# Hyena filters on Trainium2: forward and backward weights multiplied once each in two row halves of the array, their sum and difference made by VectorE

## The reference, cut to what matters

```python
def hyena_filters(L, w1, b1, w2, b2, w3, freq):
    ...
    h = (h @ w3.astype(F32)).reshape(L, HY_ORDER, 2, D_MODEL)
    ...
    return h * window[:, None, None, :]

def two_sided_fft_conv(u, h_fwd, h_bwd, bias):
    L = u.shape[1]
    kern = jnp.concatenate([h_fwd, jnp.zeros((1, h_fwd.shape[1]), F32), h_bwd[:0:-1]], axis=0)
    uf = u.astype(F32)
    spec = jnp.fft.rfft(uf, n=2 * L, axis=1) * jnp.fft.rfft(kern, n=2 * L, axis=0)[None]
    y = jnp.fft.irfft(spec, n=2 * L, axis=1)[:, :L]
    return (y + uf * bias.astype(F32)).astype(u.dtype)

def hyena_mixer(h, w_in, b_in, short_w, short_b, w1, b1, w2, b2, w3, freq, filt_bias, w_out, b_out):
    ...
    filt = hyena_filters(L, w1, b1, w2, b2, w3, freq)
    z = x1 * two_sided_fft_conv(v, filt[:, 0, 0], filt[:, 0, 1], filt_bias[0])
    z = x2 * two_sided_fft_conv(z, filt[:, 1, 0], filt[:, 1, 1], filt_bias[1])
    return z @ w_out + b_out
```

## Time and profile before

| | us |
|---|---|
| time, median of 3 runs | 2646.16 |
| lowest and highest of them | 2643.12, 2646.53 |
| the profiled execution, its own time | 2648.7 |
| span of the profiled execution | 2646.3 |
| mean granted TensorE clock, share of full speed | 0.969 |
| PE busy over the span | 2461.9 (93%) |
| DVE busy over the span | 1141.1 (43%) |
| ACT busy over the span | 773.5 (29%) |

### The profile page before, as it was taken

One profiled execution on the slowest core, in us unless ns is written; L12 is line 12 of the kernel. 1 busy time (PEld: TensorE's weight loads), 2 busy tenths in 40 slices (PEclk: granted clock), 3 DMA queues, 4 the chain that ended last, 5 costly groups with the idle time before them and its releaser, 6 DMA issues. The chain is left out here.

```text
span 2646.3 us, 39564 instructions
## 1 busy us (share of the span) xinstructions
PE 2461.9 (93%) x16812; PEld 1555.6 (59%) x16812; DVE 1141.1 (43%) x2226; ACT 773.5 (29%) x1602; POOL 51.5 (2%) x68
## 2 busy tenths in 40 slices
PE   8989999999899999978799999998999969988887
PEld 7856888888678888855443334344767743322222
DVE  4456543333788989886300000002556542211113
ACT  4346433333433333223311111112347522110002
POOL 0000000000000000000200000000000010000000
PEclk9979999999999999987899999999999979999999
DMA  5240332222210101025799999997230479999996
GB/s 205 97 153 29 143 116 96 96 96 96 94 50 33 50 33 50 32 112 203 313 383 397 377 384 386 393 384 320 101 159 2 191 258 367 428 428 428 427 428 284
DMA packets 58103, 570.49 MB, mean 216 GB/s; under 512 B 6815, under 2 KB 15015, under 8 KB 24776
## 3 DMA queue, kind: packets, MB, share of 16 engines
q1 hardware_dynamic: 50904, 544.37, 51.5%
q0 software_dynamic: 5584, 18.35, 2.2%
q10 hardware_dynamic: 1440, 5.24, 0.5%
HBM read 554.84 MB, written 13.11 MB: 215 GB/s over the span
## 5 line engine op out<-in xcount | busy, mean ns | idle before, releaser
L2973 PE MATMUL moe_gate<-ring,moe_xe_l 128*32 128x512 f32 (+1 forms) x1240 | 192.6, 599 | 17.8 <-DMA ring<-in_moe_gu 11.9
L3960 DVE SCALAR_TENSOR_TENSOR moe_hidden<-moe_hidden,moe_gate_rows,moe_up 128x512 f32<-128x512 f32 x31 | 23.2, 747 | 400.4 <-ACT moe_hidden L3883 400.4
L2973 PE MATMUL moe_up<-ring,moe_xe_l 128*32 128x512 f32 (+1 forms) x1240 | 190.2, 594 | 0.0
L3988 DVE SCALAR_TENSOR_TENSOR residual<-experts_psc,mod,residual 128x512 f32<-128x512 f32 (+1 forms) x76 | 53.3, 707 | 283.9 <-PE experts_psc L3824 169.1
L3744 PE MATMUL experts_py_l<-ring,experts_turn_l 128*32 128x512 f32 (+1 forms) x1136 | 141.3, 593 | 3.5 <-DMA ring<-in_moe_down 2.8
L1019 DVE TENSOR_TENSOR mlp_w_lo<-ring,mlp_w_hi 128x512 fp32r<-128x512 f32 x144 | 96.7, 688 | 97.8 <-ACT mlp_w_hi L964 97.6
L3883 ACT ACTIVATE moe_hidden<-moe_gate 128x512 f32<-128x512 f32 x31 | 18.5, 597 | 360.2 <-PE moe_up L2973 360.2
L964 ACT CAST mlp_w_hi<-ring 128x512 fp32r<-128x512 f32 x144 | 86.4, 618 | 123.5 <-PE mlp_acc L920 123.5
L2973 PEld LDWEIGHTS moe_up<-ring,moe_xe_l 128*32 128x32 f32 (+1 forms) x1240 | 49.7, 115 | 108.2 <-issue 108.2
L2973 PEld LDWEIGHTS moe_gate<-ring,moe_xe_l 128*32 128x32 f32 (+1 forms) x1240 | 44.8, 115 | 99.9 <-issue 70.1
L918 PE MATMUL mlp_acc<-mlp_h_hi,mlp_w_hi 128*128 128x512 f32 x256 | 100.0, 391 | 0.0
(11 more groups left out here) (678 smaller groups left out, 5210.5 us busy)
## 6 DMA issues: line engine op xcount, KB each, us to landing
ring<-in_moe_gu SPq DMA_DIRECT2D x91, 2048.0 KB, 11.3
ring<-in_moe_down SPq DMA_DIRECT2D x45, 2048.0 KB, 9.8
ring<-in_ada_w SPq DMA_DIRECT2D x24, 2048.0 KB, 8.6
ahead_wide_early<-in_moe_gu SPq DMA_DIRECT2D x9, 2048.0 KB, 30.5
ahead_wide_high<-in_moe_gu SPq DMA_DIRECT2D x9, 2048.0 KB, 30.5
ahead_wide_low<-in_moe_gu SPq DMA_DIRECT2D x9, 2048.0 KB, 30.4
normed<-in_moe_gu SPq DMA_DIRECT2D x9, 2048.0 KB, 30.5
ring<-in_w_up SPq DMA_DIRECT2D x8, 2048.0 KB, 7.4
```

Of the source, the lines that this page charges most:

```text
L2973: last = core.nc.tensor.matmul(banks[m][at:at + n, :], xe_l[:, e, k, a:a + n], columns(2 * kk + m, FH * half, FH), start=(k == 0), stop=(k ...
```

## The change: one product per side, and the sum and difference on DVE

`w3` now holds the forward weights in rows 0 to 63 and the backward weights in rows 64 to 127, once each. `filters` takes two tiles at a time: four matmuls of 64 rows by 256 columns, of which those of the upper rows write the forward side into one bank and those of the lower rows the backward side into another. `turn_filters_round` and one DMA a turn are gone. `make_taps` multiplies two banks by the window for each pair of tiles, and the new `sides` makes sum and difference in place: the first instruction adds the backward side to the forward one, the second takes twice the backward side from that sum, the third adds the bias to one row.

```diff
-        w3 = st.sb("w3", [P, 2, 2, QC])
+        w3 = st.sb("w3", [P, 2, QC])
...
-        win_loaded = st.counter("hy_win_loaded", 96 * TURNS)
+        win_loaded = st.counter("hy_win_loaded", 80 * TURNS)
...
-                        sp.wait_ge(sp_free.handle, sp_free.at(4 + spec_at(q - 1, 18 + 5)))
+                        sp.wait_ge(taps_made.handle, taps_at(q - 1, 1, 4))
...
-                        sp.dma_start(w3[0:64, :, s, :], last_layer[:, :, 0, :]).then_inc(win_loaded.handle, 16)
-                    sp.dma_start(w3[64:P, :, 0, :], last_layer[:, :, 1, :]).then_inc(win_loaded.handle, 16)
+                        sp.dma_start(w3[64 * s:64 * (s + 1), :, :], last_layer[:, :, s, :]).then_inc(win_loaded.handle, 16)
...
                 def filters(it, o, some=range(6)):
-                    for t in some:
-                        b = take_spec(it, 18 * o + t)
-                        nc.tensor.matmul(b[:], h2[:, t * P:(t + 1) * P], w3[:, o].rearrange("p s n -> p (s n)"), start=True, stop=True).then_inc(sp_done.handle, 1)
-
-                def transform(it, m0, src):
+                    for t in some[::2]:
+                        both = [take_spec(it, 18 * o + t + s) for s in range(2)]
+                        for i in range(2):
+                            for s in range(2):
+                                side = slice(64 * s, 64 * (s + 1))
+                                last = nc.tensor.matmul(both[s][:, i * QC:(i + 1) * QC], h2[side, (t + i) * P:(t + i + 1) * P], w3[side, o, :], start=True, stop=True, tile_position=(64 * s, 0))
+                                if i:
+                                    last.then_inc(sp_done.handle, 1)
+
+                def transform(it, m0, src, made):
...
+                            if a == 0 and s in made:
+                                pe.wait_ge(taps_made.handle, made[s])
...
                 def spectra(it, o):
-                    pe.wait_ge(sp_free.handle, sp_free.at(4 + spec_at(it, 18 * o + 5)))
-                    transform(it, 18 * o + 6, lambda a: taps[:, a])
+                    transform(it, 18 * o + 6, lambda a: taps[:, a], {0: taps_at(it, o, 0), 2: taps_at(it, o, 4)})
...
-                turn_filters_round(0)
...
-                        turn_filters_round(it + 1)
...
                 def make_taps(it, o, some=range(6)):

-                    for t in some:
+                    for t in some[::2]:
                         m = 18 * o + t
-                        if t == 5:
-                            dve.wait_ge(sp_free.handle, sp_free.at(4 + spec_at(it, m - 1)))
-                            if o:
-                                dve.wait_ge(win_loaded.handle, win_loaded.at(96 * (it + 1)))
-                            zero = taps[0:1, 0, 0:5:4, :]
-                            link(nc.vector.tensor_tensor(zero, zero, at_zero[:].unsqueeze(1).to_broadcast([1, 2, QC]), ALU.add))
-                        dve.wait_ge(sp_done.handle, sp_done.at(spec_at(it, m)))
-                        nc.vector.tensor_tensor(taps[:, :, t, :], spec[m % 4][:].rearrange("p (s n) -> p s n", s=2), win[:, t].unsqueeze(1).to_broadcast([P, 2, QC]),
-                                                ALU.mult).then_inc(sp_free.handle, 1)
+                        dve.wait_ge(sp_done.handle, sp_done.at(spec_at(it, m + 1)))
+                        for s in range(2):
+                            last = nc.vector.tensor_tensor(taps[:, s, t:t + 2, :], spec[(m + s) % 4][:].rearrange("p (t n) -> p t n", t=2), win[:, t:t + 2, :], ALU.mult)
+                            last.then_inc(sp_free.handle, 1)
+
+                def sides(it, o, first, n):
+
+                    dve.wait_ge(sp_free.handle, sp_free.at(4 + spec_at(it, 18 * o + first + n - 1)))
+                    ahead, behind = [taps[:, s, first:first + n, :] for s in range(2)]
+                    link(nc.vector.tensor_tensor(ahead, ahead, behind, ALU.add))
+                    link(nc.vector.scalar_tensor_tensor(out=behind, in0=behind, scalar=-2.0, in1=ahead, op0=ALU.mult, op1=ALU.add))
+                    dve.wait_ge(win_loaded.handle, win_loaded.at(80 * (it + 1) if o else 80 * it + 64))
+                    zero = taps[0:1, 0, first, :]
+                    nc.vector.tensor_tensor(zero, zero, at_zero[:], ALU.add).then_inc(taps_made.handle, 1)
...
                         make_taps(0, 0)
+                        sides(0, 0, 0, 4)
+                        sides(0, 0, 4, 2)
...
                         add_out(it - 1, 5)
+                        sides(it, 0, 0, 4)
                         add_out(it - 1, 6)
+                        sides(it, 0, 4, 2)
                         add_out(it - 1, 7)
...
                     make_taps(it, 1, range(4))
+                    sides(it, 1, 0, 4)
                     convolve(it, 4)
                     convolve(it, 5)
                     make_taps(it, 1, range(4, 6))
+                    sides(it, 1, 4, 2)
```

More of the change, by code:

```diff
@@ L2311, in spec_at, with taps_at @@
             return it * SP + m + 1
+        def taps_at(it, o, first):
+            return taps_made.at(4 * it + 2 * o + (2 if first else 1))
         def out_chunk(it):
@@ L2496, in _ @@
                     if it == 0:
-                        pe.wait_ge(turned_round.handle, turned_round.at(1))
+                        pe.wait_ge(win_loaded.handle, win_loaded.at(64))
                         filters(0, 0)
@@ L2645, in gated_high @@
                         nc.scalar.copy(u_hi[:, j, 0:UP - 2], u[:, 4 + j, 0:UP - 2]).then_inc(u_high.handle, 1)
-                def turn_filters_round(it):
-                    act.wait_ge(win_loaded.handle, win_loaded.at(96 * it + 80))
-                    nc.scalar.activation(w3[64:P, :, 1, :], w3[64:P, :, 0, :], ACT.Identity, scale=-1.0).then_inc(turned_round.handle, 1)
                 weights_high(-1, 0)
```

8 lines of the change are left out of this document (4 added, 4 removed).

## The result

The changed kernel takes 2656.6 us (median of 6 runs, 2655.4 to 2659.1) against 2646.0 (6 runs, 2639.1 to 2650.5): slower, ratio 1.0042 (95% interval 1.0028 to 1.0055), 10.6 us. The forecast was 2655.1, 8.9 us slower.

The account below looks back on a forecast made before the run. PE and DVE were taken to hand the lead to each other, DVE's slack being 3.05 + 3.49 us in turn 1. Turns 0 to 3 add 2.9 + 2.1 + 2.5 + 1.4 = +8.9 to 2646.2: 2655.1 us, range 2653.0 to 2660.6.

Parts of the forecast that it names:

- Prices: Filters of four tiles 2.1 us on PE, of two 1.25; `sides` 2.84 and 1.78 on DVE; linked steps 1.25 and 0.72.
- DVE's waits used up, the rest passed on to PE: Beside the outward products, turns 1 to 3: 3.79 us more on DVE against 3.05 of waits; second transposes 1.6 later.
- ACT's cast: At the turn's end: outward products wait for this cast, so about 0.5 of PE's 1.3 us filter saving arrives.
- The clock: PE's clock falling at three new waits, 1.5 us each; counted only in the upper end of the range.
- Turn 0: +2.9 us at the turn's end, +3.9 if the third pair of tiles waits for banks at a slow clock.
- PE's lead: Turn 0, first order: gates wait 2.08 us for PE, so its 1.3 saving counts and +2.0 reaches the second order.
- Turn 3: +1.4 us: 1.6 - 1.31 in the first order, 4.0 - 2.91 in the second.
- Between the orders: The second order's four-tile filters get 1.3 us shorter, but DVE runs without a gap and takes nothing from it.
- R1: Rival: PE bounds nearly everywhere, DVE's 7.8 us a turn fit its 14; 14 us gained, 2632; chance 0.10.
- the +14.4 at the top of the range: Whole kernel: one more us in turn 0 and the clock falling at three new waits, giving 2660.6 us.

Follow-up runs that it names:

- run 2: Kernel before, with DVE's new steps at the changed kernel's places and waits, filters and ACT's negation as they were: 2661.7 us, ratio 1.0060.
- run 3: Changed kernel, PE filling its waits before token transposes and the context tiles' unit with unused products in turns 1 to 3: 2651.3 us, ratio 1.0025.
- run 1: Changed kernel without the sum and difference on DVE, bias row kept: 2628.8 us, ratio 0.9937 to the kernel before.
- run 10: Changed kernel, GpSimd making first-order `sides` (turns 1 to 3) and eight low weight parts a turn, short convolutions moved later, turn 0's `sides` split: 2637.0 us.
- run 6: Kernel before, with eight low parts of the projection weights a turn made by GpSimd instead of DVE: 2637.8 us, ratio 0.9974.
- run 7: As run 5, and GpSimd also makes sum and difference of the first order's four latent tiles in turns 1 to 3: 2659.6 us, ratio 1.0047.
- run 5: Changed kernel, with eight of twelve low parts of the projection weights a turn made by GpSimd instead of DVE: 2668.0 us, ratio 1.0087.

## Why the prediction was right, and where its steps were off

- **Prices: right.** Filters 1.93 and 1.07 (2.1 and 1.25 forecast), with 3.4 less PE time a turn (3.5), `sides` 2.85 and 1.78 (2.84 and 1.78). Linked steps cost what the rows said: 1.25 and 0.72 from start to start.
- **DVE's waits used up, the rest passed on to PE: right.** The second transposes start 1.73 later in their turn than before (855.74 to 860.81, less the 3.34 by which the turn began late); +1.6 was forecast. The reason for it, PE's gain waited away, is run 2 against the changed kernel. The waits before the second transposes (0.53 to 1.77) and at unit 2 (1.91) are those named. One reading on the way was wrong: the first outward product does not wait for ACT's cast of the earlier trace rows. It begins 1.82 behind the gate step (837.18), 2.84 before, and ahead of that cast's end (836.82 + 0.84), so 1.0 us of PE's gain arrives there and not 0.5. The end did not come earlier by it, since DVE was behind.
- **The clock: mis-sized.** The sum left it out, and the range counted it three times. It fell behind the first order's waits in turns 1, 2 and 3, and in turn 1 in the second order too (4.14 for twelve records, 917.49); behind the same wait of 1.91 in turn 2 it stayed (2.75 for twelve). Run 3 got 5 us back, and its four turns are 9.3 longer than before, where the sum without the clock had 8.9. In the table the clock is half of the +3.24 that stands against +1.6. The row for it was there, and the case that waits of 0.94 and 1.77, 2.7 together, do what one of 2.77 had done stood only in the range.
- **Turn 0: the upper bound was the value**, +4.05 against +2.9, with +3.9 as the bound. The step that failed is PE's lead: 1.3 from the filters and 0.65 from ACT were taken off the first order, and run 1, which has both and no additions, is only 0.3 shorter there (50.79 against 51.08). The third pair of tiles waits 2.61 us for banks and runs at the lower clock (2.08 us for eight records, 1.13 in turn 1), in run 1 as well. The additions cost 3.6 of the 3.9 forecast (54.41 less 50.79).
- **Turn 3: right in sum, +1.6 against +1.4, wrong in its parts.** The first order lost 2.0, 1.5 of it through the clock (run 3: 63.91 against 65.45), and the second gained 0.4.
- **Between the orders, "takes nothing from it": only half right.** It holds with the additions in place. Run 1 shows that without them PE's saving counts almost in full, so R1's price was near (2632 against 2628.8), and so was its condition: the additions must find room. Run 10 makes that room in turns 1 and 2, 2.5 us each below run 6, but over the whole kernel no gain over run 6 is left that is clear of the noise (2637.0 and 2637.8).
- **The total was closer than its parts, and that is luck.** The four turns took 14.1 more, not 8.9, close to the +14.4 at the top of the range; the profile of after had 5.8 less behind the stage, of which the forecast knew nothing, and the medians lie 10.6 apart.

## What to carry to other kernels

Before a saving on one engine is paid for on another, walk the chain and ask which of the two the other waits for in each stretch: here shorter filters were worth 16 us with DVE's load unchanged and about 5 with the price put on DVE. Price the clock with each new wait of PE, not only the wait. Work moved to an idle engine has to be placed by what the busy one reads at that time: beside steps that read PSUM GpSimd cost DVE nothing (run 7), beside steps that read SBUF alone it cost DVE 2.9 us for the 2.4 that it took over (run 5). And when a relief makes a change pay, try the relief without the change: run 6, without it, is as fast as run 10 within the noise.
